# Block one's attention: the scaling of the exponentials by the reciprocal of their sum on GpSimd, in four buffers

## The reference, cut to what matters

```python
def _masked_softmax(logits, mask):
    logits = jnp.where(mask, logits.astype(jnp.float32), NEG_BIG)
    m = jnp.max(logits, axis=-1, keepdims=True)
    p = jnp.where(mask, jnp.exp(logits - m), 0.0)
    return p / jnp.maximum(jnp.sum(p, axis=-1, keepdims=True), TINY)
...
        p_c = _masked_softmax(s_c, cmp_end[None, :] <= t[:, None])
        o_c = jnp.einsum('bghqn,bngd->bqghd', p_c, vc)
...
        p_s = _masked_softmax(s_s, m_s).reshape(bsz, B_GROUPS, B_HPG, NSA_QBLOCK, topk, SEL_BLOCK)
        o_s = jnp.einsum('bghqkl,bgqkld->bqghd', p_s, v_sel)
...
        p_w = _masked_softmax(s_w, m_w)
        o_w = jnp.einsum('bghqk,bkgd->bqghd', p_w, vwb)
...
        return gb[:, :, 0, :, :, None] * o_c + gb[:, :, 1, :, :, None] * o_s + gb[:, :, 2, :, :, None] * o_w
```

## Time and profile before

| | |
|---|---|
| median of 3 runs | 2839.66 us (2835.14 to 2841.67) |
| span of the profiled execution | 2840.7 us |
| TensorE busy | 2750.5 us, 97%, 16512 matmuls |
| TensorE weight loads | 2340.8 us, 82% |
| VectorE busy | 1782.5 us, 63%, 3037 instructions |
| ScalarE busy | 1065.5 us, 38% |
| GpSimd busy | 193.3 us, 7%, 184 instructions |

### The profile page before, as it was taken

How to read it: one execution, slowest core, us unless ns; L and a number is a source line. 1 busy time by engine, 2 the same in 40 slices (tenths; PEclk the granted TensorE clock), 3 DMA queues, 4 the chain that set the end, 5 groups by cost and what they waited for, 6 DMA issues and landing times.

```text
span 2840.7 us, 45223 instructions
## 1 busy us (share of the span) xinstructions
PE 2750.5 (97%) x16512; PEld 2340.8 (82%) x16512; DVE 1782.5 (63%) x3037; ACT 1065.5 (38%) x1690; POOL 193.3 (7%) x184
## 2 busy tenths in 40 slices
PE   8999999999999999999999999999999999899998
PEld 8669999579988888775777788888788888688998
DVE  7466556576666565687675666555655557756665
ACT  5356544356442221325434322222322214554443
POOL 0000000000000000031213000000000000144000
PEclk9999999999999999999999999999999999999999
DMA  5535544635544443321432334443344333245554
GB/s 193 187 125 179 184 157 162 215 122 183 181 147 143 146 146 126 118 78 51 139 130 71 100 134 140 148 135 131 133 141 148 134 133 118 79 129 159 167 179 157
DMA packets 118649, 401.16 MB, mean 141 GB/s; under 512 B 12928, under 2 KB 20992, under 8 KB 118144
## 3 DMA queue, kind: packets, MB, share of 16 engines
q1 hardware_dynamic: 115408, 392.48, 41.4%
q10 hardware_dynamic: 3120, 7.07, 0.7%
HBM read 398.45 MB, written 1.05 MB: 141 GB/s over the span
## 4 chain that ended last, share of the span: by engine, by line
PE 85%; DVE 5%; issue 4%; DMA 2%; ACT 2%; POOL 1%; DVEq 1%; ACTq 0%; SPq 0%; POOLq 0%
PE bank L835 24%; PE bank L842 23%; PE bank L839 23%; PE bank L1571 2%; DMA ring<-weights 2%; PE bank L2004 1%; DVE w_lo L796 1%; PE bank L2363 1%; PE bank L2357 1%; PE bank L2360 1%; DVE work L2125 1%; DVE hn_lo L1056 1%; PE bank L933 1%; POOL w_lo L796 1%; PE bank L1493 1%
## 5 line engine op out<-in xcount | busy, mean ns | idle before, releaser
L772 ACT ACTIVATE w_hi<-ring 128x1024 fp32r<-128x1024 f32 (+1 forms) x548 | 572.5, 1046 | 1196.3 <-DMA ring<-weights 1195.5
L796 DVE TENSOR_TENSOR w_lo<-ring,w_hi 128x1024 fp32r<-128x1024 f32 (+1 forms) x538 | 658.3, 1225 | 543.2 <-ACT w_hi L772 539.6
L839 PE MATMUL bank<-hn_hi,w_hi 128*128 128x256 f32 (+1 forms) x2816 | 883.4, 333 | 0.0
L842 PE MATMUL bank<-hn_lo,w_hi 128*128 128x256 f32 (+1 forms) x2816 | 883.2, 333 | 0.0
L842 PEld LDWEIGHTS bank<-hn_lo,w_hi 128*128 128x128 f32 x2816 | 535.3, 190 | 52.2
L839 PEld LDWEIGHTS bank<-hn_hi,w_hi 128*128 128x128 f32 x2816 | 535.2, 190 | 52.1
L835 PE MATMUL bank<-hn_hi,w_lo 128*128 128x256 f32 (+1 forms) x2816 | 546.6, 336 | 9.5 <-DVE w_lo L796 6.4
L835 PEld LDWEIGHTS bank<-hn_hi,w_lo 128*128 128x128 f32 x2816 | 440.3, 190 | 70.7 <-issue 12.4
L839 PE MATMUL bank<-hid_hi,w_hi 128*128 128x512 f32 (+1 forms) x704 | 248.7, 362 | 0.0
L842 PE MATMUL bank<-hid_lo_a,w_hi 128*128 128x512 f32 (+1 forms) x640 | 226.2, 362 | 0.0
L963 DVE SCALAR_TENSOR_TENSOR conds<-ring,con 128x1024 f32<-128x1024 f32 x106 | 130.9, 1235 | 49.8 <-DMA ring<-weights 32.4
(11 more groups left out here) (339 smaller groups left out, 3189.1 us busy)
## 6 DMA issues: line engine op xcount, KB each, us to landing
ring<-weights SPq DMA_DIRECT2D x694, 512.0 KB, 3.4
ring<-weights SPq DMA_DIRECT2D x32, 384.0 KB, 3.0
ring<-weights SPq DMA_DIRECT2D x32, 256.0 KB, 2.9
ring<-weights SPq DMA_DIRECT2D x28, 192.0 KB, 2.3
con<-consts ACTq DMA_DIRECT2D x1, 2063.0 KB, 9.7
con<-consts ACTq DMA_DIRECT2D x1, 1088.0 KB, 5.0
res<-ctx_cm ACTq DMA_DIRECT2D x1, 1024.0 KB, 5.7
con<-params ACTq DMA_DIRECT2D x1, 1024.0 KB, 7.3
```

The costliest lines, as they stand in the source:

```text
L772: act.activation(w_hi[:, slot, 0:w], ring[slot][:, 0:w], ACT.Copy).then_inc(s.w_hi, 1)
L796: eng.tensor_tensor(w_lo[slot][:, 0:w], ring[slot][:, 0:w], w_hi[:, slot, 0:w].bitcast(F32), ALU.subtract).then_inc(s.w_lo, 1)
L839: pe.matmul(dst, high, x_hi(k), start=False, stop=False)
L842: return pe.matmul(dst, high, x_lo(k), start=False, stop=(stop and k == order[-1]))
```

## The change

The two scalings per unit, and the one of a `cmp` unit, move from VectorE to GpSimd, in a loop of its own behind the layer's other GpSimd work (`attention_pool`, `unit_scale`). VectorE's last small operation now signals a new semaphore att_r, and GpSimd signals att_p. The exponentials go to four buffers `ex` (2048 columns that the carve of the work buffer had left without a name) in place of the two of `pr`; ScalarE's exponential waits for the transposes of the unit four back, not two. VectorE's normalisation gains a wait for the scaling of the unit two back, since the reciprocals still have two places.

```diff
 SLOTS = 4
+EX = 4
@@
+        self.att_r = sem("att_r")
@@
-        (sm_b, pr_b, pt_b, rstd, lnb, fa_b, _, vtok_b, sg, kc, sga, mix_b, ada_row) = carve(
+        (sm_b, pr_b, pt_b, rstd, lnb, fa_b, ex_b, vtok_b, sg, kc, sga, mix_b, ada_row) = carve(
             work, [1024, 1024, 1024, 512, 512, 2048, 2048, 1792, 512, 512, 512, 2048, 512])
@@
+        ex = ex_b.rearrange("p (u k) -> p u k", u=EX)
@@
-                mm = pe.transpose(bank[6][0:heads_n, 0:P], pr[:, x.u % 2, 0:heads_n], ident)
+                mm = pe.transpose(bank[6][0:heads_n, 0:P], ex[:, x.u % EX, 0:heads_n], ident)
             else:
                 for c in range(2 * x.kt):
-                    mm = pe.transpose(bank[6][:, c * P:(c + 1) * P], pr[:, x.u % 2, c * P:(c + 1) * P], ident)
+                    mm = pe.transpose(bank[6][:, c * P:(c + 1) * P], ex[:, x.u % EX, c * P:(c + 1) * P], ident)
@@ unit_norm
             dve.wait_ge(s.att_e, x.u + 1)
+            if x.u >= 2:
+                dve.wait_ge(s.att_p, x.u - 1)
@@
-                dve.tensor_tensor(c_rcp, c_rcp, gate[:, x.tt, 0:QH], ALU.mult)
+                dve.tensor_tensor(c_rcp, c_rcp, gate[:, x.tt, 0:QH], ALU.mult).then_inc(s.att_r, 1)
+                return
+            last = dve.reciprocal(rcp[:, at:at + 2], smu[:, at:at + 2])
+            if x.kind != "fox":
                 dve.drain()
-                dve.tensor_tensor(p_u, p_u, c_rcp.unsqueeze(2).broadcast_to([P, QH, N_CMP]),
-                                  ALU.mult).then_inc(s.att_p, 1)
+                c0 = (8 if x.kind == "slc" else 16) + 4 * x.g + 2 * x.j
+                last = dve.tensor_tensor(rcp[:, at:at + 2], rcp[:, at:at + 2], gate[:, x.tt, c0:c0 + 2], ALU.mult)
+            last.then_inc(s.att_r, 1)
+
+        def unit_scale(pool, x):
+
+            pool.wait_ge(s.att_r, x.u + 1)
+            if x.kind == "cmp":
+                p_u = ex[:, x.u % EX, 0:heads_n].rearrange("p (h k) -> p h k", h=QH)
+                pool.tensor_tensor(p_u, p_u, c_rcp.unsqueeze(2).broadcast_to([P, QH, N_CMP]),
+                                   ALU.mult).then_inc(s.att_p, 1)
                 return
-            dve.reciprocal(rcp[:, at:at + 2], smu[:, at:at + 2])
-            dve.drain()
-            if x.kind != "fox":
-                c0 = (8 if x.kind == "slc" else 16) + 4 * x.g + 2 * x.j
-                dve.tensor_tensor(rcp[:, at:at + 2], rcp[:, at:at + 2], gate[:, x.tt, c0:c0 + 2], ALU.mult)
-                dve.drain()
+            at = 2 * (x.u % 2)
             for hh in range(2):
                 c = slice(hh * x.keys, (hh + 1) * x.keys)
-                last = dve.tensor_scalar(pr[:, x.u % 2, c], pr[:, x.u % 2, c], rcp[:, at + hh:at + hh + 1], None,
-                                         ALU.mult)
+                last = pool.tensor_scalar(ex[:, x.u % EX, c], ex[:, x.u % EX, c], rcp[:, at + hh:at + hh + 1], None,
+                                          ALU.mult)
             last.then_inc(s.att_p, 1)
@@ unit_exp
-            if x.u >= 2:
-                act.wait_ge(s.att_t, x.u - 1)
+            if x.u >= EX:
+                act.wait_ge(s.att_t, x.u - EX + 1)
@@
-                last = act.activation(pr[:, x.u % 2, c], half_scores(x, hh)[:, 0:x.keys], ACT.Exp, scale=x.scale,
+                last = act.activation(ex[:, x.u % EX, c], half_scores(x, hh)[:, 0:x.keys], ACT.Exp, scale=x.scale,
@@ block1_pool
+            attention_pool(pool, units_block1(l))
+
+        def attention_pool(pool, units):
+            for x in units:
+                unit_scale(pool, x)
```

More of the change, by code:

```diff
@@ L1194, in unit_norm @@
             dve.wait_ge(s.att_e, x.u + 1)
+            if x.u >= 2:
+                dve.wait_ge(s.att_p, x.u - 1)
             at = 2 * (x.u % 2)
             if x.kind == "cmp":
-                p_u = pr[:, x.u % 2, 0:heads_n].rearrange("p (h k) -> p h k", h=QH)
+                p_u = ex[:, x.u % EX, 0:heads_n].rearrange("p (h k) -> p h k", h=QH)
                 dve.tensor_tensor(p_u, p_u, cmask[:, x.tt, :].unsqueeze(1).broadcast_to([P, QH, N_CMP]), ALU.mult)
@@ L1205, in unit_norm @@
                 dve.drain()
-                dve.tensor_tensor(c_rcp, c_rcp, gate[:, x.tt, 0:QH], ALU.mult)
+                dve.tensor_tensor(c_rcp, c_rcp, gate[:, x.tt, 0:QH], ALU.mult).then_inc(s.att_r, 1)
+                return
+            last = dve.reciprocal(rcp[:, at:at + 2], smu[:, at:at + 2])
+            if x.kind != "fox":
                 dve.drain()
-                dve.tensor_tensor(p_u, p_u, c_rcp.unsqueeze(2).broadcast_to([P, QH, N_CMP]),
-                                  ALU.mult).then_inc(s.att_p, 1)
-                return
-            dve.reciprocal(rcp[:, at:at + 2], smu[:, at:at + 2])
-            dve.drain()
-            if x.kind != "fox":
-                c0 = (8 if x.kind == "slc" else 16) + 4 * x.g + 2 * x.j
-                dve.tensor_tensor(rcp[:, at:at + 2], rcp[:, at:at + 2], gate[:, x.tt, c0:c0 + 2], ALU.mult)
-                dve.drain()
+                c0 = (8 if x.kind == "slc" else 16) + 4 * x.g + 2 * x.j
[4 more added lines that the diff above has]
+            if x.kind == "cmp":
+                p_u = ex[:, x.u % EX, 0:heads_n].rearrange("p (h k) -> p h k", h=QH)
+                pool.tensor_tensor(p_u, p_u, c_rcp.unsqueeze(2).broadcast_to([P, QH, N_CMP]),
+                                   ALU.mult).then_inc(s.att_p, 1)
+                return
+            at = 2 * (x.u % 2)
             for hh in range(2):
                 c = slice(hh * x.keys, (hh + 1) * x.keys)
-                last = dve.tensor_scalar(pr[:, x.u % 2, c], pr[:, x.u % 2, c], rcp[:, at + hh:at + hh + 1], None,
-                                         ALU.mult)
+                last = pool.tensor_scalar(ex[:, x.u % EX, c], ex[:, x.u % EX, c], rcp[:, at + hh:at + hh + 1], None,
+                                          ALU.mult)
             last.then_inc(s.att_p, 1)
@@ L1232, in unit_exp @@
             act.wait_ge(s.att_m, x.u + 1)
-            if x.u >= 2:
-                act.wait_ge(s.att_t, x.u - 1)
+            if x.u >= EX:
+                act.wait_ge(s.att_t, x.u - EX + 1)
             if x.kind == "cmp":
-                act.activation(pr[:, x.u % 2, 0:heads_n], c_sm[:, 0:heads_n], ACT.Exp).then_inc(s.att_e, 1)
+                act.activation(ex[:, x.u % EX, 0:heads_n], c_sm[:, 0:heads_n], ACT.Exp).then_inc(s.att_e, 1)
                 return
```

## The result

The changed kernel takes 2854.06 us (median of 5 runs, 2853.82 to 2854.66), the kernel before 2839.66 (5 runs, 2835.14 to 2843.36). The ratio is 1.0052, 95% interval 1.0041 to 1.0063: 14.4 us slower, where +2.6 was forecast and the range ended at 2848. The profiled execution of the changed kernel took 2853.82 us with a span of 2851.9.

The account below looks back on a forecast made before the run. TensorE, busy 97% of the span, was taken as the bound. 2 layers x 4 x 0.32 us gave +2.6 us, other edits 0; on the 2839.66 median, forecast 2842.3 us, range 2837 to 2848.

Parts of the forecast that it names:

- the price of GpSimd's scaling: Second attention half: a unit's two 128x256 scalings on GpSimd, priced from its cast, take 0.96 us.
- D: Growth per unit of the piece from VectorE's small multiply to TensorE's transposes: 0.75 to 1.07 us, +0.32 us.
- The slower rival: Same eight spots: GpSimd's scaling costs its two-input price, +6.7 us, or +7.5 (2847 us) with contention; chance 0.24.
- The count: Second attention half, units numbered 0 to 21 per layer: delays accumulate at transposes of 12, 14, 17, 20, to 4D per layer.
- the third at unit 17: Second attention half: the transposes of unit 17 were to be the third place where the delay grows, reaching +3D.
- unit 21: Last unit of each layer's attention: its transposes wait for ScalarE's copy of unit 20 and only move along, +4D.
- four buffers and VectorE's new wait: Attention exponentials and reciprocals: the older waits already cover both edits, each worth 0.
- the first half: Attention units with 128 keys: 1.64 us of slack against at most D + 0.14, counted 0.
- the hand-over out of GpSimd: Semaphore step from GpSimd's scaling to TensorE's transposes, priced at 0.05 us.
- The one into GpSimd: Semaphore step from VectorE's small multiply to GpSimd's scaling, priced at 0.06 us from a ScalarE hand-over.
- The faster rival: Second attention part: VectorE set the pace, so unloading it gives up to -3 us, 2836.7; chance 0.08.
- some 25: VectorE's busy time lost with the scalings: 80 x 0.318 us, some 25 us.

Follow-up runs that it names:

- the kernel with both waits filled: Changed kernel plus unused TensorE identity products ahead of the waits of units 12 (five) and 20 (seven) alone; 2850.14 us, ratio 1.0035.
- the one-head kernel: Changed kernel with each unit's head 0 scaled on VectorE and head 1 on GpSimd; 2842.72 us, ratio 1.0016.

## Why the prediction was wrong

**The step that failed is the price of GpSimd's scaling**, "two in full with the 0.16 us ...: 0.96 us". The pair took 1.83 us, and so D was 1.23 and not 0.32. I took the cast because it too reads one tensor, and took the two-input operation as the end above. Neither holds: the form with a scalar from memory is dearer than that with a second tensor (0.925 against 0.73 us for 256 columns, and the two-input form measured here does 512 in 1.04). Why, no run shows. The bound "from above" was a guess about the kind of operation, and the range rested on it. The slower rival named the right doubt ("arithmetic with a scalar from memory, which no row prices") and the right point of decision (0.67 us), but its own price was too low by the same bound.

**A term was missing: TensorE's clock.** I counted waits at their length, without a reason for leaving the clock out. The longest wait for a scaling in this stretch was 0.60 us before. With D = 1.23 they grew to 1.48 and 1.86, and half clock behind them made the second halves 6.8 us longer in the profiled execution (3.95 and 2.85; the stretch behind unit 20 runs on to about 208 us, past the end of the second half at 205.59, and that rest isn't in the 6.8). The term does not vanish with a small D either: at D = 0.43 the clock was 1.00 in both second halves, at D = 0.46 it fell once, for 1.4 us. It belonged in the range of this forecast, which lengthened waits of TensorE.

**The count was right.** Four places per layer, the later ones carrying the earlier ones' delay. In the kernel with both waits filled the distances between transposes grew by 1.10 us to unit 12, 1.25 to unit 14, 1.26 to units 16 and 17 together and 1.25 to unit 20, against 0.08 at 15 and nothing at 13, 18 and 19. I had the third at unit 17; it falls mostly on 16, since D is longer than the slack I had in mind. One thing more: 0.37 us at unit 21, where GpSimd has two units' scalings in a row. I let that unit wait for ScalarE only.

With the measured prices the sum is 2 x (4 x 1.23 + 0.37) = 10.6 us; the kernel without half clock measured 11.1 above the kernel before. Half clock adds 3.9 us by the medians (2854.06 less 2850.14; 3.3 by the distances to each one's kernel before) and 6.8 by the profiles. One profile shows one execution, and the rest of the program varies: the profiled second halves account for 17.1 us, the spans of the profiled executions differ by 11.2 and the medians by 14.4. Behind the second layer's attention, which no edit touches, the profiles of the fourteen kernels last 2238.5 to 2244.6 us, and stretches of half clock come and go there: at 2360 to 2380 us the granted clock was 0.69 in the profile of before and 0.98 in that of after. So the split of 14.4 us is some 10.6 for the piece and about 4 for the clock, the second known to a few us only.

**Costed at nothing, and nothing it was:** four buffers and VectorE's new wait (0.9999), the first half (0.9999), the hand-over out of GpSimd (0.05 us). The one into GpSimd took 0.10 and not 0.06, from VectorE instead of ScalarE. **The faster rival fell:** VectorE lost a third of its busy time in the second half (17.7 to 12.3 and 12.0 us), and the stretch became longer; and one turn later, with all scalings still on VectorE, TensorE hardly waited (14.59 of 14.60 us busy). Over the whole program VectorE lost 20.2 us and not "some 25": 80 times the median of one operation counts the overlap in each pair twice. The Trainium skill's GPSIMD Engine Reference, section Performance versus the Vector engine, puts elementwise work at roughly twice VectorE's time. It had the sign of the case and was nearer than my row; the trace has 3.0 times for a pair of 256 columns with a scalar (1.83 us against 0.61), 2.6 times for a single one (0.925 against 0.351), and 1.7 times for both heads in one two-input operation (1.04 against 0.61).

## What to carry to other kernels

A price bounded by another kind of operation is no bound: when an engine gets a form that no row of it shows, the range has to reach well past the dearest row, and the form itself is a choice (here a broadcast second tensor cost 1.04 us where two scalar forms cost 1.83). Work moved to an idle but slower engine needs an order of the waiting engine that gives it a turn more; the same two operations lost 14 us against the kernel before on the path and nothing one turn later. But the later order is to be tried by itself too: here it gave some 3 us (ratio 0.9983 to 1.0001) with everything on VectorE, and moving work to GpSimd on top of it brought nothing that can be told. And a longer wait on TensorE can cost more than its length: look at the granted clock behind it.

## What the runs showed of the hardware that was not expected

- GpSimd's multiply with a per-partition scalar: 0.605 us for 128 columns, 0.925 for 256, so 2.5 ns for each further column. Its two-input multiply: 0.39 us for 120 columns, 0.61 for 256, 1.04 for 512, so 1.7 ns per column.
- Waits of TensorE of 1.47 to 1.86 us, in a stretch otherwise busy, were followed in 6 of 10 cases by several us at 1.2 GHz, and one of 0.70 us was. Where unused products filled 1.2 us of the 1.48, no fall followed in 4 of 4 cases, and the time fell. One such fall cost the second half 0.8 to 2.9 us.
- VectorE and GpSimd hold each other off only in part. In the one-head kernel GpSimd's scaling lasts 0.129 us longer than alone for 256 columns and 0.066 for 128, VectorE's no longer. VectorE's own scaling takes 0.067 us more for 128 more columns (0.351 against 0.284). So GpSimd loses about as long as VectorE spends on the columns, by this estimate 0.134 and 0.067 us, and not the 0.35 and 0.28 of the whole operation. That this is the cause isn't shown by a run of its own.
- The reverse is rare. In the changed kernel two small operations of VectorE last until the GpSimd operation beside them (187.15 + 1.83 = 188.98) has ended:

```profile
188.61 0.39 DVE L1193 TENSOR_SCALAR small<-small 128x2 f32<-128x2 f32 x1
188.72 0.28 DVE L1213 RECIPROCAL small<-small 128x2 f32<-128x2 f32 x1
```

At 590.97, in the second layer, one takes 0.21 us and ends with GpSimd's operation as well. Elsewhere in the same trace the same two, at 172.38 and 172.49, take 0.17 us each in the middle of a run of GpSimd's scalings. The Trainium skill, SBUF — State Buffer, section SBUF: two separate sides, describes the shared port pair as a lock held for a whole instruction, on VectorE's side by operations in a 2-port mode or with two inputs in SBUF. The first place agrees with that; the second does not show it, nor do the two scalings that start together and take 0.35 and 1.06 us above. What decides between them stays open.
